# A hybrid decoder block on one core: the last batch's down weights loaded and multiplied in two sets of 256 columns

## The chip, the core and the metric

The kernel runs on one core of one Trainium2 chip. The metric is device time in microseconds, the median of three runs. Engines are named as in the profile: PE (TensorE), DVE (VectorE), ACT (ScalarE), POOL (GpSimd), SP (SyncE, which here issues nearly all loads and stores).

## The reference

One decoder layer over 256 tokens of width 1024, in float32: two token mixers, then a mixture of experts, then a final norm. The change lies in the last part of the mixture.

```python
def hierarchical_moe(h, w_rg, b_rg, w_re, b_re, w_gate, w_up, w_down):
    ...
    def expert(acc, inp):
        wg, wu, wd, c = inp
        hid = jax.nn.silu(h @ wg) * (h @ wu)
        return acc + (hid @ wd) * c[..., None].astype(h.dtype), None

    out, _ = lax.scan(expert, jnp.zeros_like(h), (w_gate, w_up, w_down, jnp.moveaxis(combine, -1, 0)))
    return out

def reference(...):
    ...
        x = x + hierarchical_moe(h, ...)
    return rmsnorm(x, norm_final)
```

There are 32 experts with 256 hidden columns each; a token goes to two of them. `w_down` of one expert is 256 x 1024 floats, 1 MB.

## The kernel before

The mixture runs in rounds; a round takes up to 32 tokens of every expert, and one round is enough unless an expert has more. A round goes through the 32 experts in 8 batches of 4. In a batch PE multiplies the gathered tokens of each expert by its gate and up weights (`gate_up`, 2 MB an expert), turns the result (`turn`), and multiplies the hidden values by the down weights (`down(h)`, h = 0 or 1, one half of 512 output columns each). The four experts of a batch stand side by side: each uses 32 columns of the PE array, so four matmuls, one from each expert, run at the same time, and their results fill the four groups of 32 rows of one PSUM bank. A float32 matmul appears in the trace as two records, which the text calls passes; `down(h)` is 2 x 4 matmuls, 16 records, in four steps of four.

A half's result is copied to `o_sb` (ACT copies half 0, DVE copies half 1, at L2073) and then multiplied by the selection weights `selWT` and added to the four output banks: bank 4 (tokens 0 to 127, columns 0 to 511), bank 5 (the same tokens, columns 512 to 1023), bank 6 and bank 7 (the other tokens). In the last batch these four sums are `final_sum(t, h)` (recorded at L1103), and each increments `sums_complete`.

After the last batch ACT squares each of the four banks in the order `SUMMED` (L1504, with a read of the accumulator behind it), and DVE in its own order runs: the copy of half 1; a load of the number of rounds into a register and a branch on it; `weighted(0)` and `weighted(1)` (L2146, banks 4 and 6 times the norm weight); `mean_square(0)` (L2139); `weighted(2)` (bank 5); `mean_square(1)` (L2139, which needs the square of bank 7). POOL turns the mean squares into scales (L649), DVE and ACT apply them, and SP stores the result.

SP issues the loads in one order written out by hand. `reload_dw(b)` issues the down weights of batch b: first all four first halves, then all four second halves, each a transfer of 512 KB whose 128 rows are 4 KB of contiguous memory, into eight buffers (`DW`; those of the last batch are named xs, x, queries_and_attention and attention_small). Each half of each buffer has its own semaphore `s_dw[i][h]`. The gate and up weights are transfers of 2 MB with rows of 16 KB.

PSUM banks 0 to 3 are handed out round robin in the order of `SEG`; `start(job)` waits until the bank is empty and `out(job)` until its result is copied.

Of the kernel before, what the change touches and what calls it, by code (L numbers as in the profile page):

```python
# [12 lines left out]
P = 128  # L13
D, S = 1024, 256
KT = D // P
TT = S // P
# [9 lines left out]
C = 32  # L26
BE = P // C
NB = NE // BE
# [96 lines left out]
SUMMED = ((0, 0), (1, 0), (0, 1), (1, 1))  # L125
SEG = dict(first=GATHER_N, body=BATCH_C + GATHER_N + DOWN_C, last=BATCH_C + DOWN_C)

# [20 lines left out]
def build(nc, a, out):  # L148
    with ExitStack() as ctx:
# [3 lines left out]
        def sem(name):  # L153
            return ctx.enter_context(nc.semaphore(name))
# [114 lines left out]
        selWT = m0[:, 512:768]  # L269
# [43 lines left out]
        s_sq, s_xn, s_xr, s_w = sem("squares_summed"), sem("x_normed"), sem("expert_input_done"), sem("selection_weights_ready")  # L313
        s_wr = sem("router_weights_scaled")
        s_nffn, s_nr = sem("ffn_norm_loaded"), sem("rounds_ready")
        s_sel, s_tanh = sem("selection_ready"), sem("expert_tanh")
# [89 lines left out]
        def step_full(*at):  # L406
            k, n = place(*at)
            return full[k], n + 1
# [19 lines left out]
        def _(sp):  # L428
# [34 lines left out]
            def first_dw(e, halves=range(2)):  # L463
                load_dw(e % NDW, e % BE, e - e % BE, halves)
# [46 lines left out]
            def reload_dw(b):  # L511
                for h in range(2):
                    sp.wait_ge(*step_full("body", f"O{h}.c", 0, b - 2))
                    for j in range(BE):
                        first_dw(b * BE + j, (h,))

            def first_round():
# [11 lines left out]
            def one_round(r):  # L529

                if isinstance(r, int):
                    first_round()
                    return
                sp.wait_ge(*step_full("last", "O1.c", r - 1))
                for j in range(BE):
# [117 lines left out]
        def _(pe):  # L653
# [448 lines left out]
            def add(q, l, r, s, e, w=512):  # L1102
                return nc.tensor.matmul(bank[4 + q][:, 0:w], l, r, start=s, stop=e, skip_group_check=True)  # L1103
            def steps(seg, r, b, weights):
# [102 lines left out]
                def final_sum(t, h):  # L1207
                    add(2 * t + h, selWT[:, t * P:(t + 1) * P], o_sb[:, h, :], False, True).then_inc(s_sum, 1)
                down(0)
                out("WT.c")  # L1210
                out("O0.c")
                final_sum(0, 0)
                down(1)
                final_sum(1, 0)
                out("O1.c")
                final_sum(0, 1)
                final_sum(1, 1)

# [293 lines left out]
        def _(dve):  # L1512
# [554 lines left out]
            def steps(seg, r, b):  # L2067
# [49 lines left out]
                if seg == "body":  # L2117
                    dve.wait_ge(*step_full(seg, "WT.c", r, b))
                    select_weights(n + 1, b + 1)
                    gathered()  # L2120
                out_of("O1.c", o_sb[:, 1, :])

# [95 lines left out]
```

## Time and profile before

| | us |
|---|---|
| median of 3 runs (lowest, highest) | 510.57 (509.75, 511.38) |
| the profiled execution, its own time | 510.2 |
| its span | 508.3 |
| PE busy | 464.4 (91%) |
| DVE busy | 224.2 (44%) |
| ACT busy | 90.0 (18%) |
| mean granted clock of PE | 0.972 of 2.4 GHz |

All times in the rows are microseconds from the start of the span. The profile is of one execution. Busy times add up over the whole kernel, whereas the change touches only about the last 20 us, so the rows below are almost all of that stretch. "PEclk" or a granted clock of 1.00 is 2.4 GHz and 0.50 is 1.2 GHz.

### The profile page before, as it was taken

The numbers are of one execution on the slowest core, as the hardware profiler recorded it, in microseconds if no ns is written. First come the engines' busy times: TensorE is split into PE (matmuls) and PEld (weight loads), VectorE is DVE, ScalarE is ACT, GpSimd is POOL, SyncE is SP. The second block draws the span as 40 slices with busy tenths as digits, with TensorE's granted clock in tenths as the row PEclk, the third lists the DMA queues.
The fourth block names the chain that finished last, engine by engine and source line by source line (L and its number), as shares of the span: only waits on it lengthen the run. The fifth ranks groups of instructions, "written<-read, shape, count | busy, mean of one in ns | idle before, by whom it ended". The sixth has DMA issues, their size and how long they took to land.

```text
span 508.3 us, 6257 instructions
## 1 busy us (share of the span) xinstructions
PE 464.4 (91%) x2434; PEld 249.8 (49%) x2434; DVE 224.2 (44%) x512; ACT 90.0 (18%) x244; POOL 41.0 (8%) x62
## 2 busy tenths in 40 slices
PE   5999999999999999986999889999999979679683
PEld 2499744554555545532444746465463626244231
DVE  1553029828757688756894542223131212111113
ACT  1000015214440110100003612111021201011022
POOL 0600050400000001000502200000000000000001
PEclk9999999999999999998999989999999999989877
DMA  8998679225034039596087899999999999999962
GB/s 267 412 369 200 211 267 392 104 91 242 1 143 188 0 139 413 213 410 229 21 318 276 328 422 427 406 431 430 407 431 415 419 431 411 430 409 431 417 269 85
DMA packets 20859, 151.32 MB, mean 298 GB/s; under 512 B 2947, under 2 KB 3396, under 8 KB 14172
## 3 DMA queue, kind: packets, MB, share of 16 engines
q1 hardware_dynamic: 19296, 147.88, 71.9%
q0 software_dynamic: 1296, 2.92, 2.9%
q8 instruction: 22, 0.36, 0.3%
q10 hardware_dynamic: 236, 0.08, 0.1%
q14 instruction: 9, 0.07, 0.0%
HBM read 148.25 MB, written 2.62 MB: 297 GB/s over the span
## 4 chain that ended last, share of the span: by engine, by line
PE 71%; DMA 14%; DVE 6%; SPq 5%; issue 2%; ACT 0%; POOLq 0%; POOL 0%; DVEq 0%; ACTq 0%
PE bank L670 35%; PE bank L695 26%; DMA attention_small<-in_moe_down 6%; DMA ring<-in_moe_gate_up 5%; SPq L458 4%; PE bank L1103 4%; PE bank L1130 3%; PE bank L701 2%; DMA ring<-in_dense 2%; SPq L454 1%; DVE nsa L1880 1%; DVE ring L1619 0%; DVE nsa L1884 0%; DVE nsa L1531 0%; DVE rt L1531 0%
## 5 line engine op out<-in xcount | busy, mean ns | idle before, releaser
L2073 DVE COPY nsa<-bank 128x512 f32<-128x512 f32 x32 | 22.1, 691 | 105.2 <-PE bank L670 84.2
L695 PE MATMUL bank<-ring,x 128*128 128x512 f32 x128 | 57.3, 594 | 0.0
L670 PE MATMUL bank<-ring,nsa 128*32 128x512 f32 x336 | 44.5, 653 | 8.6 <-DMA ring<-in_moe_gate_up 8.6
L695 PE MATMUL bank<-ring,hT_and_y 128*128 128x512 f32 x112 | 50.5, 596 | 0.0
L1465 ACT ACTIVATE nsa<-bank 128x512 f32<-128x512 f32 (+1 forms) x40 | 22.2, 555 | 125.4 <-PE bank L670 105.9
L670 PEld LDWEIGHTS bank<-cst,nsa 128*128 128x128 f32 x256 | 31.4, 197 | 24.7 <-issue 19.2
L695 PEld LDWEIGHTS bank<-ring,x 128*128 128x128 f32 x128 | 23.8, 190 | 27.6 <-issue 27.5
L670 PE MATMUL bank<-cst,nsa 128*128 128x32 f32 x256 | 34.1, 283 | 1.2 <-DVE nsa L2073 1.2
L695 PEld LDWEIGHTS bank<-ring,hT_and_y 128*128 128x128 f32 x112 | 20.6, 190 | 24.0 <-issue 23.9
L1103 PE MATMUL bank<-nsa 128*128 128x512 f32 x64 | 30.8, 622 | 0.8 <-ACT nsa L1465 0.8
L2083 DVE SCALAR_TENSOR_TENSOR cst<-cst,bank 128x64 f32<-128x64 f32 x32 | 7.1, 221 | 53.4 <-ACT cst L1473 53.4
L1130 PE MATMUL bank<-nsa,Tb 128*128 128x128 f32 x256 | 30.2, 276 | 0.3 <-DVE nsa L1998 0.3
L1130 PEld LDWEIGHTS bank<-nsa,Tb 128*128 128x128 f32 x256 | 29.3, 192 | 0.4 <-issue 0.4
L670 PE MATMUL bank<-hT_and_y,ring 128*128 128x256 f32 x128 | 28.2, 380 | 0.2 <-issue 0.2
L670 PEld LDWEIGHTS bank<-hT_and_y,ring 128*128 128x128 f32 x128 | 24.1, 190 | 4.0 <-DVE hT_and_y L1550 0.8
L670 PEld LDWEIGHTS bank<-ring,nsa 128*32 128x32 f32 x336 | 9.5, 113 | 30.7 <-issue 19.5
L670 PE MATMUL bank<-ring,Tb 128*128 128x512 f32 x32 | 17.2, 698 | 5.7 <-DMA ring<-in_dense 5.7
L670 PE MATMUL bank<-ring,hT_and_y 128*128 128x128 f32 (+2 forms) x96 | 22.0, 388 | 0.0
L1694 DVE CUSTOM_DVE_ANT_0 nsa<-bank,Tb 128x128 f32<-128x128 f32 (+1 forms) x32 | 9.6, 354 | 28.1 <-DMA Tb<-bias_rows 26.1
L1103 PEld LDWEIGHTS bank<-nsa 128*128 128x128 f32 x64 | 11.5, 193 | 20.3 <-issue 19.7
L1614 DVE TENSOR_TENSOR ring<-ring 128x2048 f32<-128x2048 f32 (+1 forms) x7 | 15.0, 2137 | 11.1 <-PE bank L695 11.1
L670 PE MATMUL bank<-xs,cst 128*32 128x512 f32 x32 | 16.7, 658 | 2.9 <-DMA attention_small<-in_moe_down 2.9
(283 smaller groups left out, 666.5 us busy)
## 6 DMA issues: line engine op xcount, KB each, us to landing
ring<-in_moe_gate_up SPq DMA_DIRECT2D x21, 2048.0 KB, 20.0
ring<-in_dense SPq DMA_DIRECT2D x17, 2048.0 KB, 11.7
hT_and_y<-in_moe_gate_up SPq DMA_DIRECT2D x6, 2048.0 KB, 20.7
vr_and_gr<-in_moe_gate_up SPq DMA_DIRECT2D x5, 2048.0 KB, 22.4
windows<-in_moe_down SPq DMA_DIRECT2D x8, 512.0 KB, 19.4
nsa<-in_moe_down SPq DMA_DIRECT2D x8, 512.0 KB, 20.1
attention_small<-in_moe_down SPq DMA_DIRECT2D x8, 512.0 KB, 19.4
qkT<-in_moe_down SPq DMA_DIRECT2D x8, 512.0 KB, 19.5
```

The source lines that it names most:

```text
L454: sp.dma_start(GU[i].rearrange("p k w f -> p (k w f)"), expert(gate_up_v, j, e)).then_inc(s_gu[i], 16)
L458: sp.dma_start(DW[i][:, h, :, :].rearrange("p k n -> p (k n)"), expert(down_v[:, h, :, :], j, e)).then_inc(s_dw[i][h], 16)
L670: return nc.tensor.matmul(o, l, r, start=s, stop=e)
L695: ins = nc.tensor.matmul(o, l[:, k, :], r[:, k, :], start=first and k == 0, stop=last and k == n - 1, skip_group_check=True)
L701: ins = nc.tensor.transpose(o[:, i * P:(i + 1) * P], s, ident)
L1103: return nc.tensor.matmul(bank[4 + q][:, 0:w], l, r, start=s, stop=e, skip_group_check=True)
L1130: ins = nc.tensor.matmul(o[:, k * P:(k + 1) * P], xe[:, t, (4 * h + k) * P:(4 * h + k + 1) * P], selG[:, t, :, :].rearrange("p e s -> p (e ...
L1465: nc.scalar.activation(dst, bank[k][:, src], ACT.Copy).then_inc(emptied[k], 1)
L1614: V.tensor_tensor(b11, b12, b11, ALU.subtract).then_inc(s_T1, 1)
L1694: ins = V.tensor_tensor_reduce(dst, o[:, b * S:b * S + w], Tt[:, h, S - w:S], 1.0, -3e38, ALU.add, ALU.max, mx[:, t, h, b:b + 1])
L2073: V.tensor_copy(dst, bank[k][:, src]).then_inc(emptied[k], 1)
L2083: V.scalar_tensor_tensor(h, t, 1.0, bank[k][:, 0:2 * C], ALU.add, ALU.mult).then_inc(s_hch, 1)
```

## The change

In the last batch of the first round the four second halves are no longer loaded as four transfers of 512 KB but as eight of 256 KB: first columns 0 to 255 of the half for all four experts (set 0, on the old semaphores), then columns 256 to 511 (set 1, on four new ones). A row of such a transfer is two pieces of 1 KB, since the 256 columns are taken from each of the two blocks `k`. PE multiplies, DVE copies and PE sums set by set: the old `down(1)` becomes `down_columns(0)` into bank 2 and `down_columns(1)` into bank 3, each copy has 256 columns, and each of the two sums of half 1 becomes two sums of 256 columns. `sums_complete` is incremented only by the sums of set 1, so ACT's squares of banks 5 and 7 wait for both sets.

```diff
-SEG = dict(first=GATHER_N, body=BATCH_C + GATHER_N + DOWN_C, last=BATCH_C + DOWN_C)
+SEG = dict(first=GATHER_N, body=BATCH_C + GATHER_N + DOWN_C, last=BATCH_C + DOWN_C + ["O2.c"])
...
+        s_dq = [sem(f"last_down_columns{j}_loaded") for j in range(BE)]
...
             def reload_dw(b):
                 for h in range(2):
                     sp.wait_ge(*step_full("body", f"O{h}.c", 0, b - 2))
+                    if b == NB - 1 and h == 1:
+                        for q in range(2):
+                            for j in range(BE):
+                                last_columns(b * BE + j, q)
+                        return
                     for j in range(BE):
                         first_dw(b * BE + j, (h,))
+
+            def last_columns(e, q):
+
+                i, j, w = e % NDW, e % BE, slice(q * 256, q * 256 + 256)
+                rows = expert(down_v[:, 1, :, :], j, e - j).rearrange("p (k n) -> p k n", k=2)
+                sp.dma_start(DW[i][:, 1, :, w], rows[:, :, w]).then_inc((s_dw[i][1], s_dq[j])[q], 16)
...
-                sp.wait_ge(*step_full("last", "O1.c", r - 1))
+                sp.wait_ge(*step_full("last", "O2.c", r - 1))
...
+                def down_columns(q):
+                    for j in range(BE):
+                        pe.wait_ge(*(weights[j][3][1] if q == 0 else (s_dq[j], 16)))
+                    o = start(f"O{1 + q}.c")
+                    for f in range(2):
+                        for j in range(BE):
+                            ins = mm(o[j * C:(j + 1) * C, 0:256], hide[:, j, f, :],
+                                     weights[j][1][:, 1, f, q * 256:q * 256 + 256], f == 0, f == 1)
+                    end(f"O{1 + q}.c", ins)
+
+                def sum_columns(t, q):
+                    w = slice(q * 256, q * 256 + 256)
+                    return nc.tensor.matmul(bank[5 + 2 * t][:, w], selWT[:, t * P:(t + 1) * P], o_sb[:, 1, w],
+                                            start=False, stop=True, skip_group_check=True)
                 down(0)
                 out("WT.c")
                 out("O0.c")
                 final_sum(0, 0)
-                down(1)
+                down_columns(0)
                 final_sum(1, 0)
                 out("O1.c")
-                final_sum(0, 1)
-                final_sum(1, 1)
+                for t in range(TT):
+                    sum_columns(t, 0)
+                down_columns(1)
+                out("O2.c")
+                for t in range(TT):
+                    sum_columns(t, 1).then_inc(s_sum, 1)
...
-                out_of("O1.c", o_sb[:, 1, :])
+                if seg == "body":
+                    out_of("O1.c", o_sb[:, 1, :])
+                    return
+                for q in range(2):
+                    out_of(f"O{1 + q}.c", o_sb[:, 1, q * 256:q * 256 + 256], slice(0, 256))
```

On PE, at the end of the last batch, the program before stands as follows, from the first sum (bank 4) to the last (bank 7); a row is one matmul, and xs, x, queries_and_attention and attention_small hold the down weights of the four experts.

```order
L1103 MATMUL bank4<-nsa 128x512
L670 MATMUL bank2<-xs,cst 32x512
L670 MATMUL bank2<-x,cst 32x512
L670 MATMUL bank2<-queries_and_attention,cst 32x512
L670 MATMUL bank2<-attention_small,cst 32x512
L670 MATMUL bank2<-xs,cst 32x512
L670 MATMUL bank2<-x,cst 32x512
L670 MATMUL bank2<-queries_and_attention,cst 32x512
L670 MATMUL bank2<-attention_small,cst 32x512
L1103 MATMUL bank6<-nsa 128x512
L1103 MATMUL bank5<-nsa 128x512
L1103 MATMUL bank7<-nsa 128x512
```

In the changed program, at the same place, the row before these is the sum of bank 4 and the eight matmuls of set 0 into bank 2; it goes on like this.

```order
L1115 MATMUL bank6<-nsa 128x512
L1234 MATMUL bank5<-nsa 128x256
L1234 MATMUL bank7<-nsa 128x256
L682 MATMUL bank3<-xs,cst 32x256
L682 MATMUL bank3<-x,cst 32x256
L682 MATMUL bank3<-queries_and_attention,cst 32x256
L682 MATMUL bank3<-attention_small,cst 32x256
L682 MATMUL bank3<-xs,cst 32x256
L682 MATMUL bank3<-x,cst 32x256
L682 MATMUL bank3<-queries_and_attention,cst 32x256
L682 MATMUL bank3<-attention_small,cst 32x256
L1234 MATMUL bank5<-nsa 128x256
```

What moved: before, the whole second half is multiplied ahead of the sum of bank 6; now the eight matmuls of its second set stand behind that sum and behind one half-width sum of bank 5 and of bank 7, and the last copy can start only after them.

On DVE, the end of the last batch and what follows it, before:

```order
L2083 SCALAR_TENSOR_TENSOR cst<-cst,bank3 128x64
L2085 TENSOR_TENSOR cst<-cst,bank3 128x64
L2073 COPY nsa<-bank2 128x512
L418 TENSOR_LOAD nround_i
L418 ISA x2
L419 COMPARE_AND_BRANCH
```

And after the change:

```order
L2114 SCALAR_TENSOR_TENSOR cst<-cst,bank3 128x64
L2116 TENSOR_TENSOR cst<-cst,bank3 128x64
L2104 COPY nsa<-bank2 128x256
L2104 COPY nsa<-bank3 128x256
L419 TENSOR_LOAD nround_i
L419 ISA x2
L420 COMPARE_AND_BRANCH
```

One copy became two; everything that DVE does for the final norm stands behind the second.

## Rows read from the trace of the kernel before

**Rows 1.** The profile page, parts 1 and 4: busy time, chain by engine.

```profile
PE 464.4 (91%) x2434; PEld 249.8 (49%) x2434; DVE 224.2 (44%) x512; ACT 90.0 (18%) x244; POOL 41.0 (8%) x62
...
PE 71%; DMA 14%; DVE 6%; SPq 5%; issue 2%; ACT 0%; POOLq 0%; POOL 0%; DVEq 0%; ACTq 0%
```

**Rows 2.** The chain of waits, 488 to 508.3: start us, us, what.

```profile
458.48 30.37 DMA attention_small<-in_moe_down
...
489.09 3.15 PE bank L670 x16
...
492.26 0.61 ACT nsa L1465
...
493.01 2.05 PE bank L1103 x2
```

**Rows 3.** Timeline of SP, the loads' queue, 440 to 508.3: start, us, what.

```profile
459.60 1.08 SPq L458 DMA_DIRECT2D xs<-in_moe_down  x1
...
474.57 4.24 SPq L458 DMA_DIRECT2D attention_small<-in_moe_down  x1
```

**Rows 4.** DMA view, 465 to 475, packets of 16 KB.

```profile
DMA packets 294, 4.28 MB, mean 428 GB/s; under 512 B 33, under 2 KB 33, under 8 KB 33
...
attention_small<-in_moe_down SPq DMA_DIRECT2D x1, 512.0 KB, 19.3
```

**Rows 5.** DMA view, 485 to 490, packets of 4 KB.

```profile
DMA packets 556, 2.02 MB, mean 404 GB/s; under 512 B 63, under 2 KB 63, under 8 KB 556
```

**Rows 6.** DMA view, 3.7 to 4.2, packets of 1 and 2 KB.

```profile
DMA packets 65, 0.08 MB, mean 164 GB/s; under 512 B 9, under 2 KB 41, under 8 KB 65
```

**Rows 7.** Windows view: busy us of each engine, granted clock, DMA share, GB/s.

```profile
490.00:491.00 1.00, 1.00 (x8) 0.27 (x4) 0.00 (x0) 0.00 (x0) 0.00 (x0) 0.50 0.73 295
...
494.00:495.00 1.00, 1.00 (x5) 0.02 (x3) 0.00 (x0) 0.00 (x0) 0.00 (x0) 0.50 0.00 0
...
497.00:498.00 1.00, 1.00 (x9) 0.30 (x2) 0.29 (x1) 0.00 (x0) 0.00 (x0) 1.00 0.00 0
```

**Rows 8.** Timeline, 484 to 508.3, TensorE's second halves and the copy.

```profile
494.98 1.06 PE L670 MATMUL bank<-xs,cst 128*32 128x512 f32 x1
...
495.84 0.92 PE L670 MATMUL bank<-xs,cst 128*32 128x512 f32 x1
...
496.60 0.59 PE L670 MATMUL bank<-xs,cst 128*32 128x512 f32 x1
...
497.02 0.59 PE L670 MATMUL bank<-xs,cst 128*32 128x512 f32 x1
...
497.70 0.69 DVE L2073 COPY nsa<-bank 128x512 f32<-128x512 f32 x1 [9.33 <-PE bank L670]
```

**Rows 9.** Timeline of TensorE, 498.9 to 499.3: the pass after the third sum.

```profile
498.52 1.06 PE L1103 MATMUL bank<-nsa 128*128 128x512 f32 x2
```

**Rows 10.** Timeline, 484 to 508.3, the tail on DVE and ACT.

```profile
498.90 1.29 DVE L2146 TENSOR_TENSOR hT_and_y<-bank,cst 128x512 f32<-128x512 f32 x2 [0.51 <-issue]
...
500.33 0.16 DVE L2139 SCALAR_TENSOR_TENSOR st<-st 128x1 f32<-128x1 f32 x1
500.41 0.68 DVE L2146 TENSOR_TENSOR hT_and_y<-bank,cst 128x512 f32<-128x512 f32 x1
...
500.97 0.19 ACT L1504 ACTIVATION_READ_ACCUMULATOR hT_and_y<-bank 128x1 f32 x1
501.19 0.16 DVE L2139 SCALAR_TENSOR_TENSOR st<-st 128x1 f32<-128x1 f32 x1
...
502.06 2.07 SPq L548 DMA_DIRECT2D out<-hT_and_y  x3
```

**Rows 11.** Groups by form, TensorE: busy, mean ns, idle before.

```profile
L670 PE MATMUL bank<-hT_and_y,ring 128*128 128x256 f32 x128 | 28.2, 380 | 0.2 <-issue 0.2
```

**Rows 12.** Timeline of TensorE, 70 to 78: sixteen matmuls, four column groups.

```profile
77.31 1.07 PE L670 MATMUL bank<-ring,windows 128*32 128x256 f32 x16
```

**Rows 13.** Groups by form, DVE: a copy of 256 columns.

```profile
L1587 DVE COPY keys<-bank 64x256 f32<-64x256 f32 x8 | 3.4, 422 | 6.0 <-PE bank L670 5.9
```

## The prediction

> **What bounds the kernel now.** I read the page first, then the chain of waits, then the end of the span in the timeline. PE is busy 91% and makes 71% of the chain, loads 14% [rows 1]; such shares say little about the last 20 us, so the rest comes from that stretch.
>
> The last load that anything waits for is the fourth first half (attention_small): its transfer, issued at 458.48, lands at 458.48 + 30.37 = 488.85, and 0.24 us later PE starts `down(0)` [rows 2]. From there PE runs without a pause except for ACT's copy (492.26 to 492.87), which the first sum needs; that sum starts at 493.01 and `down(1)` at 494.98 [rows 2, 8]. Are the second halves late for it? Their first transfer is issued at 459.60, their last at 474.57 [rows 3], and that one lands 19.3 us after its issue, at 493.87 [rows 4]. So all of them have landed 1.1 us before PE comes to them, and DMA moves nothing from 494 to 495 [rows 7]. This is the main point: in this execution no engine waits for what the change splits.
>
> The clock matters too. PE runs at 1.2 GHz (granted 0.50) at 490 and 494 and at 2.4 GHz (1.00) at 497 [rows 7]. A step of four matmuls of 512 columns takes 495.84 - 494.98 = 0.86 us at the low level and 497.02 - 496.60 = 0.42 at the high one; the level rises between, near 496.5 [rows 8].
>
> After the product DVE copies it (497.70, 0.69 us) while PE does the sum of bank 6; the next sum starts at 498.52 [rows 8, 9]. Then, on DVE: 0.51 us of "issue" behind the copy (the register load and the branch), two products with the norm weight (498.90, 1.29), the first mean square (500.33), the third product (500.41, 0.68), the last mean square (501.19) [rows 10]. ACT's last accumulator read ends at 500.97 + 0.19 = 501.16, just before the latter. So at 501.19 DVE and ACT are level: either one, if later, moves the end. What follows, from 501.19 to 508.3, is untouched.
>
> **The change, step by step**, on the clock levels of this trace. Everything up to 494.98 is the same: the loads ahead of the second halves are issued before them and in the same order.
>
> 1. Loads. The same bytes, in packets of 1 KB instead of 4 KB, and eight issues instead of four. No row has packets of 1 KB alone. With 16 engines all busy, a 16 KB packet takes 10 x 16 / (294 - 33) = 0.613 us and a 4 KB one 5 x 16 / (556 - 63) = 0.162 us, small packets taken off [rows 4, 5]; on a line through both, 1 KB takes 0.049. The second halves are 32 packets of 4 KB for each engine, 5.2 us, so they begin about 488.7; as 128 packets of 1 KB they take 6.3. Set 0 then lands near 491.8 and set 1 near 495.0, needed at 494.98 and near 498.5 (below). The other bound, far off: at the start of the kernel packets of 1 and 2 KB moved 164 GB/s [rows 6], at which the 2.1 MB take 12.8 us, set 1 landing at 501.5. I take the line, since the queue is full at the end as in rows 4 and 5 and empty at the start. Cost on the path: nothing, hidden by PE's work up to 498.5; 3.0 us if the slow bound held. Eight issues also have to pass a full queue: the one at 474.57 took 4.24 us [rows 3] and ended at 478.8, 15 us before its landing. Even if each transfer of two pieces a row needs twice the room, the queue stays as deep in packets as now, and a full queue can't starve the engines.
>
> 2. `down_columns(0)`: 494.98; four steps of half the width at half clock, 4 x 0.43, less 0.1 as the clock rises: ends 496.6. At full clock, the same shape (four column groups, 256 columns) took 1.07 us for 16 records including the last one's tail, 0.17 (a record of 0.59 in steps of 0.42) [rows 8, 12], so 0.90 for four steps.
>
> 3. The sum of bank 6 follows. Before, the steps ended at 497.02 + 0.42 = 497.44, and the copy began 0.26 later. The sum with the gap ahead of it took 498.52 - 497.44 = 1.08 [rows 8, 9]. Now it ends at 496.6 + 1.08 = 497.7. DVE's first copy starts at 496.6 + 0.26 = 496.9 and takes 0.42 (the row of 256 columns, on 64 partitions, is the nearest [rows 13]); done 497.3, hidden by that sum. If it weren't hidden it would cost its 0.42 + 0.26.
>
> 4. Two half-width sums: four records at 28.2 / 128 = 0.22 [rows 11], 0.88 in all: 498.55.
>
> 5. `down_columns(1)`: 0.90: 499.45. This is the first place that matters: the last copy can start only now, at 499.7 instead of 497.70, because PE does the sum of bank 6 and two half sums ahead of it. It ends at 500.1 instead of 498.39: **+1.7 us**, of which the shorter copy has already given 0.27 back.
>
> 6. DVE from there. Before, the last mean square came 501.19 - 498.39 = 2.80 after the copy, 0.2 of it slack. Packed tightly it is 0.51 + 1.29 + 0.08 + 0.68 + 0.02 = 2.58 [rows 10]. So 502.7: **+1.5**. The 0.51 is uncertain. If it counts from the start of the copy (498.90 - 497.70 = 1.20), since the register load may run beside it, the sum is 499.7 + 1.20 + 2.07 = 503.0: +1.8. It can't be below 2.07 after the copy, +1.0, were it gone. I take +1.6.
>
> 7. ACT. Set 1's sums start 0.13 after the copy (as at 498.52 [rows 9]) at 500.25 and end at 501.1. Before, the last sum ended at 498.52 + 4 x 0.44 = 500.3 and the read 0.88 later. Now the two squares (at most 0.79 each) queue behind one another from about 500.9: the last read ends at 502.4 at the latest, +1.2. DVE is later, so this is hidden; it is the price (+1.2) if DVE's were smaller than I think.
>
> The sum: nothing removed from the path, +1.6 on it; 510.2 becomes 511.8 for the profiled execution. That one lies 0.4 under the median of 510.57, so the median becomes **512.2**, +0.31%.
>
> The Trainium skill (DMA: Bandwidth & Descriptors, Bandwidth) says to batch transfers to 1 MiB or more, and fits about 2.0 us plus bytes / 436 GB/s to one DMA. By that rule four transfers of 512 KB would take 12.8 us one behind another and eight of 256 KB 20.8 us. The row speaks against it: 512 KB transfers moved 404 GB/s [rows 5], their fixed part is overlapped. It is part of the rival "loads late".
>
> **The rivals.**
>
> - *DVE-bound tail at this clock, the forecast*: +1.6, 50%. With the uncertainty of +1.0 to +1.9 I give 28 of the 50 to more than 0.3% (1.53 us), about what a measurement of this kernel tells from no change.
> - *PE stays at full clock after 489*: the level fell in this trace after PE's idle time at 488, and it may fall elsewhere in another execution. Then `down(0)` ends 1.4 us sooner, the first sum ends at 492.7, and before, `down(1)` does wait, for 493.87 + 0.24 = 494.1; copy 496.0 to 496.7. After: set 0 at 492.7, sum of bank 6 to 494.7, half sums to 495.6, set 1 to 496.5, copy 496.8 to 497.2, and with 2.80 and 2.58 behind them 499.5 against 499.8: +0.3, so 510.9. The early start wins 1.4 us and the longer order loses it again. 20%.
> - *The clock falls once more near 500*, when PE pauses for the second copy (499.45 to 500.25) and the last 0.88 us of sums take twice that: ACT's end becomes 503.3, the end +2.1 to +2.5, 512.7 to 513.1. For it: the level fell after a pause of 1.2 us. Against: the pause of 0.8 us at 492.2 is no longer. 10%.
> - *Loads late*: set 1 lands after 498.3, by rule or row above up to 501.5; each us past 498.3 costs one: up to 515.2. 8%, 7 of it over 0.3%.
> - *The other side, faster*: in most executions the second halves land later than here. Before, every us past 494.74 delays `down(1)`; after, set 0 lands earlier and its product and sums are done when set 1 comes, so that only 0.90 us of product (instead of 1.75) and a copy of 0.42 (instead of 0.69) are behind the landing, and 0.22 of DVE's slack is used: 0.85 + 0.27 + 0.22 = 1.34 us gained, 509.2, if 1 KB packets cost nothing. It decides from a landing at 494.74 + 1.5 = 496.2, 2.3 us later than in this trace; nothing in the rows shows such a spread. 7%, of which 3 over 0.3%.
> - *DVE's issue time is hidden*, ACT alone is last: +1.1, 511.7. 5%.
>
> **How the numbers follow.** Slower by over 0.3%: 28 + 10 + 7 = 45%. Faster: 3%. Within: the rest, 52%. The range 510.4 to 513.3 takes in the full clock (510.9), the forecast with both bounds, the second fall of the clock, and 0.5 us of scatter of the medians below; it leaves out most of the late loads and the faster case, and the ends of the forecast's scatter. The forecast's own range is 511.4 to 512.8.
>
> **What the changed profile would show.** Right: set 0's product starts as the first sum ends, with no wait for a load; DVE's last copy starts about 2.0 us after where it started before; the last L2139 row's counterpart comes 1.3 to 1.9 us later; ACT's last read ends before it; the second halves' last landing about 1 us later. Wrong: an idle PE ahead of set 0 or set 1 with a DMA as releaser; a step of 256 columns as long as one of 512; a granted clock of 0.50 after 497, or of 1.00 from 489 on; the DVE rows following the second copy without the 0.5 us; or a first half that lands elsewhere than near 488.9, since that would move all behind it.

## The result and the profile after

The changed kernel takes 513.17 us (median of 17 runs, 510.81 to 516.70) against 511.09 us (508.63 to 512.33) of the kernel before, run beside it: ratio 1.0045, 95% interval [1.0024, 1.0065]. It is slower by about 2.3 us. Measured once more later, the ratio was 1.0024 [1.0004, 1.0044]; both together say about +1.8 us.

The chain that ended last, in the changed kernel (start, us, what). Its first rows answer to [rows 2].

```profile
460.87 30.65 DMA attention_small<-in_moe_down
...
491.76 3.23 PE bank L682 x16
...
496.85 1.00 PE bank L682 x16
497.85 1.06 PE bank L1115 x2
498.90 0.86 PE bank L1234 x4
499.76 1.05 PE bank L682 x16
...
500.83 0.42 DVE nsa L2104
...
502.04 1.29 DVE hT_and_y L2181 x2
```

The last first half lands at 460.87 + 30.65 = 491.52, and from there PE, ACT's copy of half 0 and later DVE's second copy and its products are the chain. No load stands in it behind 491.52. Before, the chain went from the last sums on PE to ACT's squares:

```profile
497.63 1.96 PE bank L1103 x4
...
499.62 0.70 ACT hT_and_y L1504 x2
```

Now it goes through the second copy and DVE's products, as step 6 of the prediction has it.

The timeline of SP with the third and the last of the eight issues (start, us), which answers to [rows 3], and then the DMA view of 489 to 496, with the last of them (last column: us from issue to landing):

```profile
463.78 20.06 SPq L527 DMA_DIRECT2D queries_and_attention<-in_moe_down  x1
...
489.58 0.95 SPq L527 DMA_DIRECT2D attention_small<-in_moe_down  x1
```

```profile
DMA packets 1975, 2.01 MB, mean 287 GB/s; under 512 B 125, under 2 KB 1941, under 8 KB 1974
...
attention_small<-in_moe_down SPq DMA_DIRECT2D x1, 256.0 KB, 7.6
```

Packets of 1 KB moved about 350 GB/s while all 16 DMA engines were busy (the mean of 287 includes their end). Set 1's last transfer, issued at 489.58, landed 7.6 us later, near 497.15, that is 5.6 us after the last first half; before it was 5.0 [rows 4]. PE came to set 1 at 499.70:

```profile
496.78 0.40 PE L682 MATMUL bank<-xs,cst 128*32 128x256 f32 x1
...
497.02 0.38 PE L682 MATMUL bank<-xs,cst 128*32 128x256 f32 x1
...
497.78 1.13 PE L1115 MATMUL bank<-nsa 128*128 128x512 f32 x2
498.74 1.03 PE L1234 MATMUL bank<-nsa 128*128 128x256 f32 x4
499.70 0.40 PE L682 MATMUL bank<-xs,cst 128*32 128x256 f32 x1
...
501.31 1.13 PE L1234 MATMUL bank<-nsa 128*128 128x256 f32 x4 [0.55 <-DVE nsa L2104]
```

These are PE's rows behind the first sum: set 0 (a step of 256 columns takes 497.02 - 496.78 = 0.24), the sum of bank 6, the four records of the first half-width sums, set 1, and the last half-width sums. None names a DMA ahead of it. The tail on DVE, which answers to [rows 10], and behind it the register load of DVE, from the view of line L419 (its length in ns, its start in us):

```profile
497.91 0.42 DVE L2104 COPY nsa<-bank 128x256 f32<-128x256 f32 x1 [6.94 <-PE bank L682]
500.83 0.42 DVE L2104 COPY nsa<-bank 128x256 f32<-128x256 f32 x1 [2.50 <-PE bank L682]
502.04 1.29 DVE L2181 TENSOR_TENSOR hT_and_y<-bank,cst 128x512 f32<-128x512 f32 x2 [0.78 <-issue]
503.25 0.15 DVE L2174 SCALAR_TENSOR_TENSOR st<-st 128x1 f32<-128x1 f32 x1
...
503.91 0.15 DVE L2174 SCALAR_TENSOR_TENSOR st<-st 128x1 f32<-128x1 f32 x1
```

```profile
L419 DVEq TENSOR_LOAD <-nround_i x1: 545/545/545, 500.8 to 500.8; - x1
```

The second copy starts at 500.83, and so does the register load; 1.21 us after that start come the products, and the last mean square is at 503.91.

**Two traces that don't start level.** A subtraction of the two profiles (503.91 - 501.19 = 2.7) would mislead. The changed kernel's trace is already 2.4 us late when the last first half is issued (460.87 against 458.48), in code that the change doesn't touch. Laid side by side, the same instructions of the two traces lie within 0.1 us of each other from 100 to 219; the changed one falls 1.7 us behind near 222, where PE ran at 1.2 GHz for 3.4 us and before at 2.4, and another 0.8 us near 240, where its low stretch lasted 6.8 us instead of 3.4. It gets 0.9 us of that back in the first sum, which runs at 2.4 GHz (495.75 to 496.78) and not at 1.2 as in the trace of before (493.01 to 494.98 [rows 2, 8]). Even counted from the start of the first down product, these two traces hide the effect: the last mean square comes at 501.19 - 489.09 = 12.10 in the one and at 12.15 in the other, since behind that start the level was low for 6.8 us in the first and for 3.4 in the second. Windows view of the changed kernel (PE busy, PEld, DVE, ACT, POOL, granted clock, DMA share, GB/s):

```profile
222.00:226.00 4.00, 4.00 (x7) 1.59 (x6) 0.00 (x0) 0.00 (x0) 0.00 (x0) 0.58 0.97 414
236.00:243.00 7.00, 5.00 (x9) 2.57 (x10) 4.68 (x5) 0.60 (x1) 0.00 (x0) 0.52 0.88 331
...
495.00:498.00 3.00, 2.25 (x19) 0.94 (x20) 0.09 (x1) 1.28 (x3) 0.00 (x0) 0.89 0.13 40
```

and of the kernel before, in the profile that predicted:

```profile
222.00:226.00 4.00, 4.00 (x11) 1.75 (x10) 0.70 (x1) 0.60 (x1) 0.00 (x0) 1.00 0.98 419
236.00:243.00 7.00, 6.71 (x15) 3.18 (x16) 3.85 (x5) 0.60 (x1) 0.00 (x0) 0.76 0.60 253
...
495.00:498.00 3.00, 3.00 (x18) 0.80 (x18) 0.29 (x1) 0.69 (x2) 0.00 (x0) 0.75 0.03 5
```

A second profile of the kernel before (the experiment before_again) happened to have its low stretches where the changed kernel has them, near 222, near 240, and then for 3.4 us from 0.44 us after the start of the first down product (0.50 in the changed kernel). In both, PE waited for the load (a first half) at that start. This is the pair to compare. Its rows:

```profile
222.00:226.00 4.00, 4.00 (x7) 1.72 (x6) 0.00 (x0) 0.00 (x0) 0.00 (x0) 0.61 0.97 407
236.00:243.00 7.00, 6.00 (x11) 2.98 (x12) 3.71 (x4) 0.60 (x1) 0.00 (x0) 0.56 0.71 294
```

```profile
490.88 0.61 PE L670 MATMUL bank<-xs,cst 128*32 128x512 f32 x1 [1.24 <-DMA attention_small<-in_moe_down]
...
494.93 1.10 PE L1103 MATMUL bank<-nsa 128*128 128x512 f32 x2 [0.79 <-ACT nsa L1465]
...
495.95 0.62 PE L670 MATMUL bank<-xs,cst 128*32 128x512 f32 x1
...
497.94 0.69 DVE L2073 COPY nsa<-bank 128x512 f32<-128x512 f32 x1 [7.78 <-PE bank L670]
...
499.14 1.29 DVE L2146 TENSOR_TENSOR hT_and_y<-bank,cst 128x512 f32<-128x512 f32 x2 [0.51 <-issue]
...
501.43 0.16 DVE L2139 SCALAR_TENSOR_TENSOR st<-st 128x1 f32<-128x1 f32 x1
```

All times below that compare tails are counted from the start of the first down product: 490.88 in before_again, 491.76 in the changed kernel. The last mean square comes at 501.43 - 490.88 = 10.55 and 503.91 - 491.76 = 12.15: **+1.60 us**, the size that the prediction gave it. POOL's last operation behind it is 0.2 us shorter (0.79 against 1.01 us), and the spans end 508.6 - 490.88 = 17.7 and 510.9 - 491.76 = 19.2 us after that start, +1.5.

### The profile page after: what moved, and what is told of

Read it like the earlier page. It is cut to its first block, busy times and chain, and to the rows that moved or that the text cites. A ratio compares the mean times of both kernels' runs of the same rounds, so it can differ in the third digit from the quotient of the medians.

```text
span 510.9 us, 6304 instructions
## 1 busy us (share of the span) xinstructions
PE 465.8 (91%) x2454; PEld 252.1 (49%) x2454; DVE 224.3 (44%) x513; ACT 89.9 (18%) x244; POOL 41.7 (8%) x62
## 4 chain that ended last, share of the span: by engine, by line
PE 57%; DMA 24%; DVE 7%; SPq 6%; issue 2%; POOL 1%; ACT 0%; DVEq 0%; POOLq 0%; ACTq 0%
PE bank L707 27%; PE bank L682 21%; DMA bias_rows<-etab 8%; DMA attention_small<-in_moe_down 6%; DMA ring<-in_moe_gate_up 5%; SPq L459 4%; PE bank L1115 3%; PE bank L1142 3%; PE bank L713 3%; DMA x<-in_x 2%; DMA ring<-in_dense 1%; DMA Tb<-bias_rows 1%; SPq L455 1%; DVE nsa L1911 1%; DVE ring L1650 0%
## 5 line engine op out<-in xcount | busy, mean ns | idle before, releaser
L2104 DVE COPY nsa<-bank 128x512 f32<-128x512 f32 (+1 forms) x33 | 22.3, 675 | 105.1 <-PE bank L682 84.1
L682 PEld LDWEIGHTS bank<-cst,nsa 128*128 128x128 f32 x256 | 31.5, 197 | 24.7 <-issue 19.2
L1115 PE MATMUL bank<-nsa 128*128 128x512 f32 x60 | 28.1, 607 | 0.8 <-ACT nsa L1496 0.8
L682 PE MATMUL bank<-xs,cst 128*32 128x512 f32 (+1 forms) x36 | 16.2, 584 | 2.9 <-DMA attention_small<-in_moe_down 2.9
## 6 DMA issues: line engine op xcount, KB each, us to landing
windows<-in_moe_down SPq DMA_DIRECT2D x8, 512.0 KB, 19.6
nsa<-in_moe_down SPq DMA_DIRECT2D x8, 512.0 KB, 20.4
qkT<-in_moe_down SPq DMA_DIRECT2D x8, 512.0 KB, 19.5
keys<-in_moe_down SPq DMA_DIRECT2D x8, 512.0 KB, 18.4
```

Of the source, the lines that this page charges most:

```text
L682: return nc.tensor.matmul(o, l, r, start=s, stop=e)
L2104: V.tensor_copy(dst, bank[k][:, src]).then_inc(emptied[k], 1)
```

## The experiments

All ratios are to the kernel before, run beside it on the same chip.

**before_again.** No edit.

> The kernel before, unchanged, to learn how its time goes with the clock of each run. The profiles of before and after are already 2.4 us apart at 458 us, in code that the change doesn't touch, because PE ran four products of the attention part at 1.2 GHz from 222.6 on in the one and not in the other. Theory 'order' (the later last copy and the DVE work behind it cost about 1.6 us, the rest of the difference is where the clock falls by chance): ratio 1.000, and its mean clocks scatter like those of the changed kernel (0.957 to 0.971), with about 2 us between runs at 0.971 and at 0.964. Theory 'clock' (the change makes the clock fall more often): its runs lie at 0.970 or above nearly all the time.

Ratio 1.0009 [0.9992, 1.0027]. Its 12 runs had mean clocks of 0.962 to 0.973, and took 512.0 us at 0.962, 511.5 at 0.965, 509.6 at 0.969 and 0.973. So the clock falls without the change too, and shifts single runs by 2 us. Over more runs the mean clocks are nearly alike: 0.967 in the 107 runs of the kernel before that stood beside the experiments, 0.966 in the 29 of the changed kernel. Among the 107, 17 runs at 0.965 took 511.0 us on average and 8 at 0.973 took 508.8; at that rate the difference of 0.001 is an estimated 0.3 us. The theory that the falls carry the slowdown is out. The changed kernel's 17 runs at about equal clock took 513.2 us (7 runs at 0.964) and 511.2 (4 at 0.971), 1.7 and 1.6 us more than the nearest of these groups.

**loads_in_sets.** Only the loads are split.

```diff
@@ reload_dw as in the change
@@ down(h)
                         pe.wait_ge(*weights[j][3][h])
+                        if seg == "last" and h == 1:
+                            pe.wait_ge(s_dq[j], 16)
```

> Only the loads are changed: eight transfers of 256 KB; PE waits for both sets and multiplies, DVE copies and PE sums as before. Theory 'order': the last set lands 5.6 us after the last first half, as in the changed kernel, instead of 5.0; PE is busy with the first half and its sum for 5.9 us after that landing when it runs at 1.2 GHz, so nothing waits: ratio 1.000 (within 0.002). If the clock is high there PE would wait up to 2 us and lose 0.6 against before. Theory 'loads' (the small packets and more issues carry the cost): 1.003 to 1.005.

Ratio 1.0015 [0.9999, 1.0032]: not told from no change, but with a cost that the trace shows:

```profile
490.73 0.65 PE L682 MATMUL bank<-xs,cst 128*32 128x512 f32 x1 [1.26 <-DMA attention_small<-in_moe_down]
...
496.39 0.59 PE L682 MATMUL bank<-xs,cst 128*32 128x512 f32 x1 [0.48 <-DMA attention_small<-in_moe_down]
...
498.38 0.69 DVE L2087 COPY nsa<-bank 128x512 f32<-128x512 f32 x1 [8.39 <-PE bank L682]
...
501.86 0.16 DVE L2153 SCALAR_TENSOR_TENSOR st<-st 128x1 f32<-128x1 f32 x1
```

PE waited 0.48 us for set 1 (its product starts only when both sets are there), whose product starts at 496.39 - 490.73 = 5.66 instead of 5.07, and the last mean square came at 11.13 instead of 10.55: +0.6. This is what the expectation names for a level that rises soon; 1 KB packets do cost, 0.6 us, where somebody waits for all of them. In the changed kernel nobody does.

**compute_in_sets.** Only product, copies and sums in sets; the four transfers of 512 KB stay.

```diff
-                    if b == NB - 1 and h == 1:
-                        for q in range(2):
-                            for j in range(BE):
-                                last_columns(b * BE + j, q)
-                        return
...
-                        pe.wait_ge(*(weights[j][3][1] if q == 0 else (s_dq[j], 16)))
+                        pe.wait_ge(*weights[j][3][1])
```

> Only product, copies and sums are done in two sets; the loads are the four transfers of 512 KB of before. Theory 'order': 1.003 to 1.005, the whole slowdown; the last DVE copy starts 2.9 to 3.0 us after the end of the first sum, and its end comes 3.1 us before the last mean square. Theory 'loads': 1.000 to 1.001.

Ratio 1.0075 [1.0054, 1.0095], from 6 runs. All of the slowdown is here without any small packet, and the theory that the loads carry it is out. It is more than the expected 1.003 to 1.005. Of the two times in the expectation neither is met as it is worded: the last copy starts 4.06 us after the first sum is through (497.34); 2.9 us is the distance between the starts of the two copies, and 3.07 us is counted from the start of the last copy, not from its end. The last mean square is at 504.47 - 491.99 = 12.48:

```profile
491.99 1.03 PE L677 MATMUL bank<-xs,cst 128*32 128x512 f32 x1 [0.83 <-ACT nsa L1491]
...
501.40 0.42 DVE L2099 COPY nsa<-bank 128x256 f32<-128x256 f32 x1 [2.50 <-PE bank L677]
...
504.47 0.15 DVE L2169 SCALAR_TENSOR_TENSOR st<-st 128x1 f32<-128x1 f32 x1
```

The low level began 0.16 us ahead of the first product here and not 0.5 behind it; two kernels with the old product in which it lay nearly so had 10.92 and 10.90 (before_padded, 0.05 behind, and before_two_copies, 0.14 ahead; both below). So the path is +1.57, as in the changed kernel; why its six runs lie another 1 us higher isn't shown (five of them had a mean clock of 0.964, and the changed kernel takes 513.2 there, this one 513.7).

**products_first.** The changed kernel with set 1's product moved up.

```diff
                 down_columns(0)
+                down_columns(1)
                 final_sum(1, 0)
                 out("O1.c")
                 for t in range(TT):
                     sum_columns(t, 0)
-                down_columns(1)
                 out("O2.c")
```

> The changed kernel with one thing moved: PE multiplies set 1 right behind set 0, ahead of the sum of bank 6 and the half-width sums of banks 5 and 7. Theory 'order': the last copy starts 2 us sooner, and both copies lie beside the sum of bank 6; ratio to before 0.999 to 1.001, so the slowdown is gone. When the clock is high set 1 may be waited for by up to 1 us. Theories 'loads' and 'clock': it stays at 1.003 to 1.005, since loads and instructions are the same.

Ratio 1.0024 [1.0006, 1.0042]; expected were 0.999 to 1.001. The profile:

```profile
488.97 0.59 PE L682 MATMUL bank<-xs,cst 128*32 128x512 f32 x1 [1.25 <-DMA attention_small<-in_moe_down]
...
496.00 0.42 DVE L2104 COPY nsa<-bank 128x256 f32<-128x256 f32 x1 [0.44 <-PE bank L682]
...
499.04 0.16 DVE L2174 SCALAR_TENSOR_TENSOR st<-st 128x1 f32<-128x1 f32 x1 [0.55 <-ACT hT_and_y L1535]
...
499.72 0.15 DVE L2174 SCALAR_TENSOR_TENSOR st<-st 128x1 f32<-128x1 f32 x1
```

The second copy starts at 7.03 instead of 9.07, 2.0 us sooner, as expected, and the last mean square comes at 10.75 instead of 12.15. So PE's order is worth 1.4 of the 1.6 us. For the 0.2 left the rows show DVE's first mean square waiting 0.55 us for ACT's square of bank 5: that bank is complete only with the third of the four half-width sums, and its square starts 9.35 us after the first down product, against 499.85 - 490.88 = 8.97 in before_again. Then 0.24% of 510 us is 1.2, of which only 0.2 lie on this path. A part of the rest stood in none of my steps: the time outside the span (a run's time less its span). It is 1.87 us in the kernel before (29 runs, 1.81 to 1.92) and in loads_in_sets (1.86), and 2.23 in compute_in_sets and products_first and 2.26 in the changed kernel (17 runs, 2.18 to 2.33): **+0.38**. The 0.6 us that are left of the 1.2 are within the interval of the ratio.

**after_again.** No edit to the changed kernel.

> The changed kernel again, unchanged, beside the three that follow. Theory 'order, plus a fixed 0.4 outside the span': 1.0035 to 1.0045 to before. Of this about 1.5 us lie between the start of the last batch's first down product and the end of the span (19.2 against 17.7 us in two executions with the clock low over the same stretch), and 0.4 us outside the span (2.26 us against 1.87 in all runs so far). If the first figure of 1.0045 was drawn up by chance clocks, this one is nearer to 1.0035.

1.0024 [1.0004, 1.0044], below what I expected; 2.27 us outside the span; the last mean square 12.20 after the start of the first down product.

**after_early_load.** DVE's register load ahead of the last batch.

```diff
+                if isinstance(r, int):
+                    dve.wait_ge(s_nr, 1)
+                    early.append(dve.value_load(nround_i[0:1, 0:1], min_val=1, max_val=ROUNDS))
                 steps("last", r, NB - 1)
...
-            rounds(dve, one_round)
+            early = []
+            one_round(0)
+            with dve.If(early[0] > 1):
...
```

> The changed kernel, but DVE loads the number of rounds into its register before the last batch instead of behind the last copy; the branch stays where it is. Step 6 of the prediction: DVE's 1.20 us from the start of the last copy to the first product with the norm weight should become about 0.5 to 0.6 (the copy of 0.42 and the branch), and the last mean square comes 0.5 to 0.6 us sooner, as ACT's last read ends then; ratio to before 0.001 below that of the changed kernel. If the 1.20 is anything else (a wait for ACT or PE) nothing moves.

Ratio 1.0034 [1.0012, 1.0056], too wide for a difference of 0.001. The profile decides:

```profile
501.30 0.42 DVE L2104 COPY nsa<-bank 128x256 f32<-128x256 f32 x1 [2.50 <-PE bank L682]
501.64 1.28 DVE L2189 TENSOR_TENSOR hT_and_y<-bank,cst 128x512 f32<-128x512 f32 x2
...
503.23 0.16 DVE L2182 SCALAR_TENSOR_TENSOR st<-st 128x1 f32<-128x1 f32 x1 [0.32 <-ACT hT_and_y L1535]
```

The products start 0.34 us after the copy's start instead of 1.21, and the last mean square is at 503.91 - 491.81 = 12.10. Against compute_in_sets, whose level lay nearly alike (12.48), that is 0.4 sooner, a bit less than expected: DVE now waits 0.32 us for ACT. So what stands as "issue" behind the copy is the register load and the branch; the load starts with the copy and runs beside it (545 ns from 500.8 in the row of L419 above), and a shorter copy shortens nothing.

**early_set0.** Set 0 is multiplied in PE's pause for ACT's copy; the register load is ahead of the last batch, by the edit of after_early_load, which the cut below leaves out.

```diff
                 down(0)
+                down_columns(0)
                 out("WT.c")
                 out("O0.c")
                 final_sum(0, 0)
-                down_columns(0)
+                down_columns(1)
                 final_sum(1, 0)
                 out("O1.c")
-                for t in range(TT):
-                    sum_columns(t, 0)
-                down_columns(1)
                 out("O2.c")
-                for t in range(TT):
-                    sum_columns(t, 1).then_inc(s_sum, 1)
+                final_sum(0, 1)
+                final_sum(1, 1)
```

> Loads in sets and products in sets, but set 0 is multiplied right behind the first half, in the pause in which PE waits for ACT's copy; set 1 behind the first sum; then the sums of full width as before; with the early register load. Theory 'order': set 0 has landed 2.7 us after the start of the first half's product, which takes 3.2, so it isn't waited for; set 1 lands at 5.4 and its product starts at 5.6, as down(1) does before, but has half the work: the last mean square comes 10.1 to 10.3 us after that start instead of 10.55, and with the 0.4 us outside the span the ratio to before is 0.999 to 1.001. Theory 'loads': above 1.003, since the small packets are still there.

Ratio 0.9988 [0.9968, 1.0007]: the slowdown is gone, a gain not shown. 

```profile
490.71 1.03 PE L682 MATMUL bank<-xs,cst 128*32 128x512 f32 x1 [0.83 <-ACT nsa L1494]
...
494.09 0.39 PE L682 MATMUL bank<-xs,cst 128*32 128x256 f32 x1
...
497.27 0.42 DVE L2102 COPY nsa<-bank 128x256 f32<-128x256 f32 x1 [1.64 <-PE bank L682]
...
500.74 0.16 DVE L2180 SCALAR_TENSOR_TENSOR st<-st 128x1 f32<-128x1 f32 x1
```

Set 0's product starts right behind the first half's (3.38 after its start), without a wait, and the last mean square comes at 10.03; kernels with the old product and the level in this place had 10.90 and 10.92. That is 0.9 us of path won, of which 0.35 are paid outside the span (2.22). It comes from the order and not from the early register load: the last copy starts 6.57 after the first down product instead of 7.44 (before_padded), and the last mean square follows 3.46 us later, as there (3.48), right behind ACT's last read.

**early_set0_whole_loads.** The same order with the four transfers of 512 KB (early_set0 with the edit of compute_in_sets).

> The order that multiplies set 0 in the copy pause, but with the four transfers of 512 KB of before. The second halves land 4.3 to 4.8 us after the start of the first down product, set 0 alone at 2.7. Theory (the split of the loads is worth something only where a product is ready to use it early): PE stops 1 to 1.5 us ahead of set 0 for a load, and the last mean square comes at 10.8 or later instead of 10.03; ratio to before 1.001 to 1.003. If the loads' split gives nothing: 0.9988.

Ratio 1.0005 [0.9982, 1.0027], at the lower end of what was expected. The wait is there:

```profile
489.15 0.78 PE L677 MATMUL bank<-xs,cst 128*32 128x512 f32 x1 [1.24 <-DMA attention_small<-in_moe_down]
...
494.15 0.38 PE L677 MATMUL bank<-xs,cst 128*32 128x256 f32 x1 [1.56 <-DMA attention_small<-in_moe_down]
```

PE stands still for 1.56 us until a transfer lands, set 0 starts at 5.00 instead of 3.38, and the last mean square comes at 11.66 instead of 10.03. The two traces differ in one more thing: here PE waited for the last first half and began as it landed, whereas in early_set0 it waited for ACT and began 1.2 us after that landing, so its loads had a start of 1 us. So 1.6 us is the most that the split of the loads is worth to this order; the runs, whose intervals overlap, lie 0.9 us apart on average (510.7 against 509.9). It is worth that only to an order that asks for set 0 early.

**early_set0_filled.** One matmul of 128x512, its result unused, in PE's pause ahead of the first halves.

```diff
+                else:
+                    o = start("O0.c")
+                    for _ in range(1):
+                        mm(o[:, 0:512], ident, gu_sb[:, 1, 0:512], True, True)
                 for j in range(BE):
                     out(f"T{j}.c")
```

> The kernel that multiplies set 0 in the copy pause, with one more matmul (128 x 512, into a bank that the first down product overwrites; its result is used by nothing) in the pause before the first halves land. In 7 profiles out of 7 PE's clock fell to 1.2 GHz within 0.6 us of the start of the first down product and stayed there for 3.4 or 6.8 us. Theory 'clock' (the level falls because of that pause): with the pause filled the level stays at 1.00 or falls elsewhere, and up to 1.5 us come off; ratio to before 0.995 to 0.998. If the fall doesn't depend on it: 0.9988 as without.

Ratio 0.9985 [0.9967, 1.0004]; mean span 507.6 as without it (507.7). In the profiled execution the clock did stay at 2.4 GHz behind the start of the first product, and its span ends 16.3 us after that instead of 17.2. Its 12 runs had a mean clock of 0.972 against 0.968, but in their time nothing is left of it. One execution without a fall isn't enough to say that the filled pause prevents it, so what makes the level fall stays open.

**before_padded, before_small_matmuls, before_two_copies.** Three edits of the kernel before, to find where the 0.38 us outside the span come from.

```diff
                 final_sum(1, 1)
+                if not isinstance(r, int):
+                    for _ in range(24):
+                        add(0, selWT[:, 0:P], o_sb[:, 0, :], False, False)
```

> The kernel before with 24 more matmuls in PE's program for a second round, which is never run. All kernels that work in sets (24 to 30 more PE instructions in the program) have 2.23 to 2.26 us of their time outside the span, those with the old product 1.86 to 1.87. Theory 'length' (a longer PE program costs time ahead of or behind the span): 2.2 us outside, ratio 1.0005 to 1.001. Rival (it comes from what runs last, DVE's and ACT's tail): 1.87 as before.

1.89 us outside, ratio 1.0005 [0.9986, 1.0023]: not the length of PE's program.

The next one has the edit of early_set0_filled with `range(12)` and 32 columns instead of one matmul of 512.

> The kernel before with twelve matmuls of 32 columns more in the pause ahead of the first halves' landing; their results are overwritten. These are run, unlike those of the padded kernel. The time outside the span was 2.22 to 2.28 us in every kernel that works in sets and 1.86 to 1.89 in the others. Theory 'executed PE instructions': 2.2 here. Rival (another part of the change: the third bank job, DVE's second copy): 1.87. In the span nothing but the clock may move: ratio 0.999 to 1.001.

1.85 us outside: not executed PE instructions either. But the ratio is 1.0056 [1.0035, 1.0077], where I expected none. The first down product starts at 493.03, 2.2 us later than in before_again (the last first half was issued 0.6 us later too), and the low level lasts 10 us from 1.2 us ahead of it. I had put twelve matmuls of 32 columns at a fraction of a microsecond; yet sixteen records of this shape, in `turn`, take 1.97 us in the trace of before, 0.12 each, and the 24 records here took 3.30 us (from 489.81) in a pause of 1.2. The loads in the pause were no longer what PE waited for.

```diff
+                if seg == "last":
+                    k, _ = place(seg, "O1.c", r, 0)
+                    dve.wait_ge(*step_full(seg, "O1.c", r, 0))
+                    V.tensor_copy(o_sb[:, 1, 0:256], bank[k][:, 0:256])
+                    V.tensor_copy(o_sb[:, 1, 256:512], bank[k][:, 256:512]).then_inc(emptied[k], 1)
+                    return
                 out_of("O1.c", o_sb[:, 1, :])
```

> The kernel before, but in the last batch DVE copies half 1 as two copies of 256 columns behind one another (one bank, no other change). It asks where the 0.36 us outside the span come from that every kernel with products in sets has (2.2 against 1.87 us), after added PE instructions, run or not, did not bring them. Theory 'DVE': 2.2 us outside the span. Rival (the third bank job of the last batch or PE's new order): 1.87. In the span: PE's next sum waits until the second copy ends, about 0.15 us later than before, and DVE's products with the norm weight follow 1.20 us after the start of the second copy, 0.35 later than before: the last mean square 10.8 to 10.9 us after the start of the first down product; ratio 1.0005 to 1.0015.

2.12 us outside the span (12 runs, 2.06 to 2.22), +0.25 against 1.87 to 1.89. Splitting DVE's copy alone brings two thirds of the term; the mechanism, and the last 0.1, stay open, since no row of a trace lies outside the span. In the span the last mean square came at 10.90, no later than in before_padded (10.92); I expected 10.8 to 10.9 as a loss, on the wrong ground: the register load started with the first of the two copies, so the second delayed nothing. Ratio 1.0008 [0.9984, 1.0031].

## Why the prediction was partly wrong

It forecast +0.31% (+1.6 us) as the likeliest and gave 52% to a change that can't be told from none. The measured change is clear of none, +0.45% [0.24, 0.65], and 513.17 lies just inside the range.

- *The step that failed: from the span to the time of a run.* The prediction adds up the path inside the span (+1.6), turns 510.2 into 511.8 with it, and puts the time outside the span at no change, without a reason. The runs show **+0.38 us** there (2.26 against 1.87). Span +1.5 and this make 1.9 us, +0.37%, within the interval of both measurements of the changed kernel (1.0045 and 1.0024). What in the change brings the term is open beyond the 0.25 us of the split copy (before_two_copies).
- *What that did to the chances.* The forecast of +1.6 lay just above the 0.3% (1.53 us) from which the prediction counts a change, so only 28 of its 50% were counted as slower. With 0.38 more nearly all of the 50 lie above: 50 + 10 + 7 make about 2 in 3 for more than 0.3%, not 45%.
- *What bounds the kernel* was right: no engine waited for what the change splits. In the changed kernel set 0's and set 1's products start without a wait for a load. The margin was thinner than in the profile that predicted: in before_again `down(1)` starts 5.07 us after the first down product and its last load lands at 4.8, 0.3 us ahead and not 1.1.
- *Step 1, loads*: right that they cost nothing on the path. The last landing moved from 5.0 to 5.6 us after the last first half, +0.6; the line through two packet sizes gave +1.1 (6.3 instead of 5.2). The fixed part of a transfer doesn't add up eight times: the 20.8 us, an estimate by a fit in the Trainium skill (DMA: Bandwidth & Descriptors, Anatomy of one DMA — SWDGE (gpsimd) path), would have put it 15 us later. The page gives that fit for transfers issued from GpSimd; SP issued these.
- *Steps 2 to 5*: right in kind. A step of 256 columns took half of one of 512, the first copy was hidden, and the last copy started 9.07 after the start of the first down product instead of 7.06: 2.0 us, as predicted. products_first, which takes back only this order, takes back 1.4 of the 1.6 us. The sum was worked out for a level that is low until 7.4 us after that start; in the two traces compared it was low only until 3.9, and the 2.0 us came out the same.
- *Step 6*: the sum held, +1.60, in part by luck. Of its two readings the higher was right: the products come 1.21 us after the start of the copy, not 0.51 after its end (after_early_load shows the register load by itself). That alone would have made +1.8; but the work behind took 503.91 - 502.04 = 1.87 us instead of the 2.07 that I put, since an operation starts a little ahead of the recorded end of the one before it (the first mean square at 503.25, the products end at 502.04 + 1.29 = 503.33). The two errors cancel.
- *The rivals.* "PE stays at full clock after 489" got 20% at +0.3 us. Its condition was met in one of the 14 profiles (early_set0_filled); in the other 13 the level was low for 3.4 us or more, from at most 0.6 us after the start of the first down product. Its price is untested, for no trace pairs the old and the new order at full clock. In before_again the level was high again from 3.9 us on, and that was not enough: `down(1)` started at 5.07, hardly later than its loads landed, so nothing was there to win, and the order cost its full 1.6.
- *The clock falls near 500*: not seen in the two profiles of the changed kernel. *Loads late* and *faster*: not seen.

## What to carry to other kernels

Splitting a load pays only where a consumer would otherwise stand waiting, and then the consumer's order must be changed to use the first part early: here the split with set 1 behind the sums cost 1.9 us, with set 0 in an existing pause nothing. Ask also what a run's time holds outside the span: here it grew by 0.38 us. When a product is cut in two, look at what its second part is queued behind, and at all that is queued behind the copy of that second part on its own engine. And before two traces are subtracted, lay them side by side at a point ahead of the change: here they were 2.4 us apart there, more than the effect, and at different clock levels behind it.

## What the runs showed of the hardware

- Time outside the span is not a constant of the launch: 1.85 to 1.89 us on average in the kernels with the old product, 2.2 to 2.3 in those with products in sets, and 2.12 with the old product and DVE's copy split in two.
- PE's granted clock falls at places that differ between executions of one kernel; in the kernel before, runs at a mean clock of 0.965 took 511.0 us and runs at 0.973 took 508.8, so that 12 runs leave an interval of 0.2%.
- Loads of the same bytes moved 404 GB/s in packets of 4 KB [rows 5] and about 350 GB/s in packets of 1 KB.
- One issue on SP's queue took 20.1 us (463.78, in the changed kernel), and the queue still was deep enough: the last issue took place at 489.58, 7.6 us before its landing, where before it was 19.3 us, and no engine waited for it.
- A register load of 0.54 us on DVE starts together with the copy issued ahead of it (500.8 in the changed kernel; in before_two_copies 499.4, with the first of the two copies).
